# Router of a two-block transformer kernel: bias remainders on GpSimd, tile 1's squares in halves, rows split in column order and gathered at a stride of four, logits in halves

## What is computed

```
h = h + mixed @ w_o
u = rmsnorm(h, g_moe)                              # 256 x 1024
logits = u @ w_router + b_router                   # 32 experts
top_logit, top_e = top_k(logits, 4)
gate = softmax(top_logit)
# each expert e, on the tokens that chose it:
hh = u[rows of e] @ w_gu[e] + b_gu[e]              # 1024 x 2048 weights
glu, lin = split(hh);  glu = min(glu, 7);  lin = clip(lin, -7, 7)
act = glu * sigmoid(1.702 * glu) * (lin + 1)
y[rows of e] += gate * (act @ w_dn[e] + b_dn[e])   # 1024 x 1024 weights
```

## Time and profile before

| | |
|---|---|
| three runs | 1410.92, 1407.99, 1409.66 us; median 1409.66 |
| profiled execution | 1409.69 us |
| its span, first to last instruction | 1408.0 us |
| mean granted clock of TensorE | 0.986 of 2.4 GHz |
| PE, PEld busy | 91%, 52% |
| DVE, ACT, POOL busy | 35%, 29%, 4% |
| read from memory | 478 MB, 341 GB/s over the span |
| chain that ended last | PE 51%, DMA 39%, DVE 5%, ACT 4% |

### The profile page before, as it was taken

One profiled execution on the slowest core, in us unless ns is written; L12 is line 12 of the kernel. 1 busy time (PEld: TensorE's weight loads), 2 busy tenths in 40 slices (PEclk: granted clock), 3 DMA queues, 4 the chain that ended last, 5 costly groups with the idle time before them and its releaser, 6 DMA issues.

```text
span 1408.0 us, 16584 instructions
## 1 busy us (share of the span) xinstructions
PE 1286.4 (91%) x6969; PEld 736.2 (52%) x6969; DVE 486.8 (35%) x730; ACT 401.4 (29%) x644; POOL 59.0 (4%) x115
## 2 busy tenths in 40 slices
PE   8999999999899889998888988888888999899998
PEld 7888433333333333433333332333324898799986
DVE  5895311112111112111111111111114687677765
ACT  5784212000110001100001000010004766655554
POOL 4001000000000000000000000000000510000000
PEclk9999899999999999999999999999999999899999
DMA  9547799999999999999999999999999964355520
GB/s 336 171 153 297 265 388 429 428 426 429 425 428 427 428 428 426 428 428 426 428 427 428 428 427 428 427 428 429 427 427 365 251 213 150 121 184 185 188 101 30
DMA packets 78474, 480.79 MB, mean 341 GB/s; under 512 B 5504, under 2 KB 40475, under 8 KB 53568
## 3 DMA queue, kind: packets, MB, share of 16 engines
q1 hardware_dynamic: 75904, 474.76, 83.4%
q0 software_dynamic: 2496, 4.96, 1.6%
HBM read 478.39 MB, written 1.31 MB: 341 GB/s over the span
## 4 chain that ended last, share of the span: by engine, by line
PE 51%; DMA 39%; DVE 5%; ACT 4%; issue 1%; DVEq 0%; SPq 0%; ACTq 0%
DMA arena<-in_w_dn_dram 37%; PE ps L1954 21%; PE ps L2376 11%; PE ps L2416 11%; DMA ring<-in_w_dn_dram 2%; PE ps L2343 1%; DVE W L1240 1%; PE ps L2432 1%; ACT W L770 1%; PE ps L2095 1%; PE ps L2038 1%; PE ps L2533 1%; ACT arena L963 0%; PE ps L2306 0%; ACT arena L913 0%
## 5 line engine op out<-in xcount | busy, mean ns | idle before, releaser
L2376 PE MATMUL ps<-ring,arena 128*64 128x512 f32 x1392 | 315.5, 595 | 12.1 <-DMA ring<-in_w_gu_dram 11.8
L2376 PEld LDWEIGHTS ps<-ring,arena 128*64 128x64 f32 x1392 | 97.0, 137 | 209.3 <-issue 179.0
L1590 DVE TENSOR_SCALAR arena<-ps 128x512 f32<-128x512 f32 x32 | 22.1, 692 | 478.2 <-PE ps L2376 478.2
L1954 PE MATMUL ps<-X,W 128*128 128x256 f32 x1464 | 177.0, 283 | 0.3 <-DVE W L1240 0.3
L1954 PEld LDWEIGHTS ps<-X,W 128*128 128x128 f32 x1464 | 176.1, 192 | 0.9 <-DVE W L1240 0.5
L1954 PE MATMUL ps<-W,X 128*128 128x512 f32 (+2 forms) x780 | 173.0, 380 | 3.2 <-issue 1.6
L1240 DVE TENSOR_TENSOR W<-ring,W 128x2048 fp32r<-128x2048 f32 (+2 forms) x64 | 144.9, 2264 | 74.9 <-ACT W L770 74.9
L2416 PE MATMUL ps<-ring,arena 128*64 128x512 f32 x648 | 146.0, 595 | 23.0 <-DMA ring<-in_w_dn_dram 23.0
L1954 PEld LDWEIGHTS ps<-W,X 128*128 128x128 f32 x780 | 141.4, 188 | 31.7 <-DVE W L1240 4.7
L976 ACT ACTIVATE arena<-arena 128x512 f32<-128x512 f32 x32 | 20.1, 629 | 458.5 <-DVE arena L1590 458.5
L2376 PE MATMUL ps<-arena 128*64 128x512 f32 x656 | 150.1, 598 | 0.0
(11 more groups left out here) (355 smaller groups left out, 1017.5 us busy)
## 6 DMA issues: line engine op xcount, KB each, us to landing
ring<-in_w_gu_dram SPq DMA_DIRECT2D x87, 2048.0 KB, 22.4
ring<-in_w_dn_dram SPq DMA_DIRECT2D x40, 2048.0 KB, 24.9
arena<-in_w_gu_dram SPq DMA_DIRECT2D x39, 2048.0 KB, 20.7
arena<-in_w_dn_dram SPq DMA_DIRECT2D x23, 2048.0 KB, 25.6
ring<-in_w_up_dram SPq DMA_DIRECT2D x22, 1024.0 KB, 5.1
ring<-in_w_in_dram SPq DMA_DIRECT2D x15, 1024.0 KB, 12.4
ring<-in_w_down_dram SPq DMA_DIRECT2D x11, 1024.0 KB, 4.9
ring<-in_w_o_dram SPq DMA_DIRECT2D x4, 1024.0 KB, 5.0
```

The lines of the kernel that those rows point to most:

```text
L1590: e.tensor_scalar(glu, whole(gb), 7.0, None, ALU.min).then_inc(s_glu, 1)
L1954: y = e.matmul(o, l, r, start=start and i == 0, stop=stop and i == 2)
L2376: y = e.matmul(ps[c * 64:c * 64 + 64, use[0], :], xs[:, k, c0:c0 + CAP], w[:, half * D + c * 512:half * D + (c + 1) * 512], start=False, s ...
```

## The change

Six edits, all at the router.

The remainders of the biases move from VectorE to GpSimd, behind its one-hot masks and ahead of the one-hots of the experts. The scaling of the router's weights moves up on VectorE, behind the two products of the "mla" rows with the softmax sums. `uhi` and `ulo` are written in column order, and both gathers (and the one of the rarely run further rounds) read them with `every_fourth`, a step of four elements. Tile 1's squares are summed in two halves, as other stages of the kernel do. VectorE's list has the turned rows, the reciprocal and both low halves of tile 0 ahead of the last add to h, and tile 1's reciprocal ahead of the logits of tile 0. TensorE turns tile 1's second half between the two halves of tile 0's logits.

```diff
+        def every_fourth(part, t, k):
+            return part[:, t, 512 * (k // 4):512 * (k // 4) + 512].rearrange("q (p i) -> q i p", i=4)[:, k % 4]
...
 # GpSimd
             e.wait_ge(*pool["eoh", 1])
+            e.wait_ge(s_bhi, 1)
+            for q in (32, 96):
+                b = bgu2[q:q + 32]
+                e.tensor_tensor(b, braw[q:q + 32], b.bitcast(F32), ALU.subtract).then_inc(s_blo, 1)
+                e.wait_ge(s_blo, 1 if q == 32 else 2)
             e.wait_ge(*BK.filled(U_o[1][1]))
...
 # ScalarE
             def rows_hi(t, c):
                 e.wait_ge(s_scale, t + 1)
                 e.wait_ge(*pair14)
-                e.activation(uhi[:, t, c].rearrange("q (i p) -> q i p", i=4), by_rows(h[:, t, c]), ACT.Copy,
-                             scale=rs[:, t:t + 1]).then_inc(s_uhi, 1)
+                e.activation(uhi[:, t, c], h[:, t, c], ACT.Copy, scale=rs[:, t:t + 1]).then_inc(s_uhi, 1)
             rows_hi(0, slice(0, 512))
-            e.wait_ge(*h_o(1, 1))
-            e.activation(junk_m, h[:, 1, :], ACT.Square, accum_out=ss[:, 1:2]).then_inc(squares.sem, 1)
+            rows_hi(0, slice(512, 1024))
+            e.wait_ge(*h_o(1, 0))
+            e.activation(junk_m[:, 0:512], h[:, 1, 0:512], ACT.Square, accum_out=ss[:, 1:2]).then_inc(squares.sem, 1)
+            e.wait_ge(*squares["moe", 1])
+            e.activation(halfc[:, 1:2], ss[:, 1:2], ACT.Identity, scale=1.0 / D, bias=epsc).then_inc(s_half.sem, 1)
             e.wait_ge(*BK.filled(U_uT[1][0]))
             e.activation(uTp[:, 2, :], whole(U_uT[1][0]), ACT.Copy).then_inc(taken[U_uT[1][0][0]], 1)
-            root(1, 1, D, squares["moe", 1])
-            rows_hi(0, slice(512, 1024))
+            e.wait_ge(*h_o(1, 1))
+            e.activation(junk_m[:, 512:1024], h[:, 1, 512:1024], ACT.Square, accum_out=ss[:, 2:3]).then_inc(squares.sem, 1)
+            e.wait_ge(*s_half["moe", 0])
+            root(1, 1, D, squares["moe", 2], ss[:, 2:3], halfc[:, 1:2])
             rows_hi(1, slice(0, 512))
             rows_hi(1, slice(512, 1024))
...
 # VectorE
+            g0 = col0[0] + rows["g_moe"][1]
+            e.wait_ge(s_wr, 16)
+            e.tensor_tensor(wr[:, :, :], wr[:, :, :], bc(cols[:, g0:g0 + KD].unsqueeze(2), [P, KD, NE]), ALU.mult)
             over_root("mla", 0, 0, 2)
...
             split(14)
             split(15)
-            e.wait_ge(s_bhi, 1)
-            for q in (32, 96):
-                ...
-            e.tensor_tensor(wr[:, :, :], wr[:, :, :], bc(...), ALU.mult).then_inc(s_wg, 1)
...
             add_o(0, 0)
             add_o(0, 1)
             add_o(1, 0)
+            turned_out(0)
+            scaled(0)
+            rows_lo(0, slice(0, 512), 1)
+            rows_lo(0, slice(512, 1024), 2)
             add_o(1, 1)
-            scaled(0)
-            turned_out(0)
             turned_out(1)
-            rows_lo(0, slice(0, 512), 1)
+            scaled(1)
             for t in range(2):
-                if t:
-                    scaled(1)
                 e.wait_ge(*BK.filled(U_l[t]))
...
             select(0)
-            rows_lo(0, slice(512, 1024), 2)
             rows_lo(1, slice(512, 1024), 4)
...
 # TensorE
             turned_rows(1, 0)
             e.wait_ge(s_wg, 1)
-            for t in range(2):
-                if t:
-                    turned_rows(1, 1)
-                claim(U_l[t])
-                for k in range(KD): ...
+            claim(U_l[0])
+            logits(0, 0)
+            turned_rows(1, 1)
+            logits(0, 1)
+            claim(U_l[1])
+            logits(1, 0)
+            logits(1, 1)
...
-                            y = e.matmul(ps[:, x[0], a * 256:(a + 1) * 256], part[:, t, k * P:(k + 1) * P], Sr[j % 2][:, t],
+                            y = e.matmul(ps[:, x[0], a * 256:(a + 1) * 256], every_fourth(part, t, k), Sr[j % 2][:, t],
```

29 lines of the change are left out of this document (13 added, 16 removed).

## The result

The changed kernel takes 1412.33 us (median of 13 runs, 1409.37 to 1418.05) against 1408.34 us before (13 runs, 1406.31 to 1410.92): a ratio of 1.0031, 95% interval 1.0024 to 1.0039. It is slower by 4 us; forecast were 1408.4 us and a range up to 1412.2. The spans of the profiled executions are 1410.6 and 1408.0 us.

What follows compares the result with a forecast made beforehand. The prediction took the expert weights' transfers, flat at 425 to 429 GB/s, as the bound, with their start set by the router. Router gains of 1.45 and 0.2 us, taken as 1.3 for the clock: 1409.7 - 1.3 = 1408.4 us; range 1405.4 to 1412.2.

Steps and rivals of the forecast that it cites:

- I take 0: Gathers' weight loads at a step of four elements: the stride was taken to cost nothing, within bounds of 0 to 4.6 us.
- paid but overlapped: Rival: strided loads in the first four gathers take 271 ns each, overlapping matmuls; 2.8 us more, 1411.2 us, chance 0.2.
- rival of 1413.0: Strided loads in the first four gathers cost in full, none hidden: 4.6 us more, 1413.0 us, chance 0.08.
- Later gathers lie under the stream ...: 0: Strided loads in gathers after the first four: engines idle for part of every expert there, so cost 0.
- No work of an engine inside that stretch can move the end: Flat weight stream, about 210 to 1060 us: transfers set the pace, so engine work inside it counts 0.
- the forecast's 136.1: VectorE's last add to h: forecast to end at 136.1 us, 0.57 us lost by waiting behind tile 0's low rows.
- kind-clock rival: Router's end: clock falls only after the logits and returns as soon after the gather; 2.9 us gained, 1406.8 us, chance 0.15.
- the forecast's 144.2: Start of the first gather: forecast at 144.2 us instead of 145.85, from gains of 1.45 and 0.2 us.
- The remainders on GpSimd: 0: Bias remainders moved from VectorE to GpSimd before the adds to h: both effects hide, 0 us.
- the forecast's case in which the split holds GpSimd: GpSimd's remainders: if VectorE's split until 126.78 holds GpSimd, they end at 131.5 us instead of 130.2; still 0.
- the rival in which GpSimd holds the adds: Adds to h: the second remainder holds the second add until 131.5, the last sum comes 1.2 us later; 1409.6 us, chance 0.05.
- The first paragraph of the prediction: Start of the weight stream: a microsecond saved in the router or first 16 gather matmuls is one at the end; only start and aftermath count.

Runs made afterwards that it cites:

- a1: The changed kernel with all gathers reading 128 adjacent columns instead of every fourth; 0.11% faster than before, 0.42% faster than the changed kernel.
- a2: The changed kernel with the stride of four in the first four gathers only, adjacent columns in the 28 later ones; ratio 1.0006 to before.
- b1: The changed kernel with adjacent columns in the first four gathers and the stride of four in the 28 later ones; 0.23% over a1.
- c4: The changed kernel with rows in gather order, last add and turned copy ahead of tile 0's low rows, remainders back on VectorE; ratio 0.9992 to before.
- a3: The changed kernel with rows written in the gather's order again and gathered from adjacent columns, all other edits kept; 0.15% slower than before.

## Why the prediction was wrong

**The step that failed first: "I take 0" for the strided weight loads.** Its own rival, paid but overlapped, had the value: 243 ns a load measured where it put 271, and 0.93 us for eight at the full clock where it put 1.0. For the four gathers on the path it gave 2.8 us, 1.0 for each of two at the full clock and 0.44 for each of two at half; measured were 2.25, 0.93 for each of the first and 0.39 for the other two together. At half clock 16 took 4.14 us, 259 ns each, where eight at the full clock took 267 each: the pace with the stride hardly goes with the clock. The argument against it, that a load takes 0.98 ns a column anyway and need not meet the limit of the others, was a guess about a resource of which no row spoke, and ScalarE's and VectorE's rows for the same stride were the nearest rows. The rule set beside it (the Trainium skill, TensorE: Matmul & The Clock Gate, "LDWEIGHTS": columns alone, 107 ns) is contradicted as to the stride: for 128 columns both, eight loads in a row took 1.01 us with adjacent columns (126 ns each) and 1.94 with a step of four. The other (the Trainium skill, Vector Engine (DVE) Microarchitecture Reference, "Measured stream behaviour on trn2", full rate only for runs of two adjacent words) holds on VectorE: 0.87 us for a slice read in pairs (two halves of 256) where step four takes 1.10. TensorE is milder than that rule: with every second word alone its gathers took 1.23 us for eight instead of 1.21.

In number the measured time is nearer to the rival of 1413.0, loads that don't hide at all, than to the 1411.2 of the overlapped ones. That is luck: on the path the loads cost what the overlapped rival says, and the rest of the loss lies in the stream, where no rival looked.

**The step that cost more: "Later gathers lie under the stream ...: 0", and with it "No work of an engine inside that stretch can move the end".** The flat GB/s row says that the transfers never stopped; it does not say with how much room. At the start the places are full and TensorE works them off at 26.6 us an expert, while the transfers bring one in about 29.4. With 0.93 us more for each expert and clock lost beside it, TensorE is 11.5 us behind a1 at the eleventh mark, SyncE's next loads wait for its places, and the transfers lose 6.1 us of their full rate. Before, PE had 51% of the chain to DMA's 39% and was busy in 91% of the span, and from the gathers to 354 us no transfer stood in the chain, while the transfers ran at 425 to 429 from 211 us on: TensorE decided there under a flat row, and the prediction did not use it. By the casts, the router and the first gathers together lost 0.38 us up to the second one, and the later gathers 3.49 from there to the last: 1408.34 + 3.87 is 1412.21, and 1412.33 were measured. That it fits to a tenth is luck, as such marks differ by a microsecond between executions; that the larger part was lost in the later gathers is borne out by a1, a2 and b1: the stride in the first four alone costs 0.17% over a1, in the later ones alone 0.23%, in all of them 0.42%, and by the casts at the last mark 1.6, 4.2 and 6.6 us.

**The router: right in kind; the size is the clock's.** 2.46 us were gained to the gather's start, 2.17 with what the clock took from the 16 matmuls (3.75 us in a1, 3.46 before); 1.3 were forecast. The last add ended at 1.46 us behind the cast, near the 1.2 that the forecast's 136.1 gives against 134.95. In this execution the fall of the clock did not take half of the last logits: they ran in 2.76 us, all at 1.00, as the kind-clock rival had it. In b1, with the same instructions, the clock fell inside them, the gather started 9.62 us behind the cast, and the gain was 1.28 us; the forecast's 144.2 is 9.25. Of the ten kernels with these instructions seven had the kind case, to which the prediction gave 0.15, and three the other. What neither had is the other end: the clock came back 4.7 us after the gather's start and not 3.0, so that all of the 16 matmuls ran at 1.2 GHz.

**The remainders on GpSimd: 0, right.** The two took 5.96 us, the first 3.48 and the second 2.40:

```profile
121.60 2.29 DVE L1253 TENSOR_TENSOR W<-ring,W 128x2048 fp32r<-128x2048 f32 x1 [2.13 <-ACT W L779]
...
126.23 2.40 POOL L720 TENSOR_TENSOR X<-arena,X 32x1024 fp32r<-32x1024 f32 x1
```

The second has the 2.41 of the forecast. The first started at 122.67, beside VectorE's split with both inputs in SBUF, which ended at 123.89, and is 1.08 us longer; it is so in all 14 kernels that have the remainders there (3.46 to 3.48 and 2.39 to 2.41). That is the forecast's case in which the split holds GpSimd: 6.1 us from the end of ScalarE's copy to the end of the second, and 6.12 were measured. They ended at 128.63, 3.5 us before the cast, the next thing that GpSimd does. The adds to h beside them took 0.69 each, so the rival in which GpSimd holds the adds is out. c4 shows no difference in the time either.

**The stream's start.** SyncE's first ring issue moved from 18.0 us behind the cast to 16.5 (16.3 in a1). Where no stride took it back the end followed, with 1.4 us between the medians: a1 is ahead by 1.70 us at the second cast and 2.73 at the last. The first paragraph of the prediction was right in this, and wrong in its "only".

## What to carry to other kernels

When a change takes a stride out of one engine's operand and puts it into another's, price it for every use of that operand, not only for those on the path in view: here eight slices, written once each, are read by 256 loads. Leave runs of two elements or a step of two where a permuted layout is needed: for 512 elements the pairs cost 0.03 us on ScalarE and 0.15 on VectorE (two instructions for one), the step of two 0.02 us for eight gather matmuls on TensorE. A flat transfer row is a statement about the present margin: before work inside it is counted as nothing, add its lengthening per stage over all stages and set it against how far the engine can lag before a slot comes free too late (about 6 us here). The chain in order of time says it sooner: where it is an engine's for long under a flat transfer row, that engine decides. And where a clock falls or comes back near the changed instructions, one execution's gain is one draw: compare several profiles of the same instructions before a cause is read from one.

## What the runs showed of the hardware

- A weight load of 128 columns of four bytes: 197 ns with adjacent columns (mean of the 256 records, which overlap), 207 with a step of two, 328 with four, 325 with eight in 224 of the 256; back to back at the full clock a load and matmul of 256 columns take 151 ns (adjacent), 154 (two), 267 to 270 (four) and 275 to 279 (eight). At 1.2 GHz the first 16 took 235 ns each with adjacent columns and 259 with a step of four: a pair with the stride takes much the same at either clock.
- The granted clock fell more often in the kernels with strided loads: 18.7 to 27.2 us lost against 1.7 to 12.0, with TensorE's busy share higher, not lower (94% against 91% before). The same instructions met the fall at 3.4 to 4.2 us or at 5.5 to 6.6 us behind the same mark, in three and in seven of ten kernels.
- GpSimd's two-input operation over 32 partitions and 1024 elements took 2.40 us, as over 128 partitions (2.41), and 3.48 where it started 1.22 us before the end of a VectorE operation with both inputs in SBUF. VectorE's adds with one input in PSUM kept their 0.69 us beside it. Its cast of 0.29 us took 0.60 beside a contiguous low row on VectorE (the second cast of the changed kernel) and 1.14 and 1.08 beside two strided ones (a3).
